# A delta-rule input projection in three-fold fp32r products, with the convolution over eight padded rows

## The reference, cut to what matters

```
def _dn_inputs(hn, n_rows, w_in, conv_w, a_log, dt_bias):
    z = hn @ w_in
    qkv = jax.nn.silu(_short_conv(z[..., :3 * DN_INNER], conv_w, n_rows))
    gate = z[..., 3 * DN_INNER:4 * DN_INNER]
    ba = z[..., 4 * DN_INNER:]
    ...
q, k, v, beta, g, gate = _dn_inputs(hn, n_rows, ...)       # 4 rows of 64 tokens
qc, kc, vc, betac, gc, gatec = _dn_inputs(hcn, 1, ...)     # one row of 256 tokens
```

## Time and profile before

| | us |
|---|---|
| median of 3 runs (lowest, highest) | 2886.16 (2881.43, 2887.08) |
| the profiled execution | 2880.9 |
| its span | 2879.1 |
| stage `dn_proj`, first matmul to the barrier | 51.95 to 229.22 |
| TensorE busy over the span | 2587.9 (90%) |
| VectorE, ScalarE busy over the span | 1914.4 (66%), 1286.8 (45%) |
| mean granted TensorE clock over the span | 0.925 |

### The profile page before, as it was taken

The page is one execution under the profiler, slowest core; times in us unless marked ns, Lnnn a source line. Parts: engine busy times, 40 slices in busy tenths (PEclk is TensorE's granted clock), DMA queues, the critical chain, the costliest instruction groups (busy, mean ns, idle before and its releaser), DMA issues. The chain is left out here.

```text
span 2879.1 us, 46266 instructions
## 1 busy us (share of the span) xinstructions
PE 2587.9 (90%) x18362; PEld 2102.2 (73%) x18362; DVE 1914.4 (66%) x2914; ACT 1286.8 (45%) x1663; POOL 41.0 (1%) x77
## 2 busy tenths in 40 slices
PE   5996799979687999999999879789999698799996
PEld 3543699957155999999999777578888586688885
DVE  2654666645997666666666565468888663588886
ACT  2112344311055444444444345257777352477774
POOL 1000000000000000000000010000000100000000
PEclk8996899999699999999999979799999897799998
DMA  6205200033866555555555552259999530399994
GB/s 256 101 29 191 78 3 3 3 125 132 322 198 214 187 185 187 189 185 187 185 186 189 187 201 82 84 219 366 367 360 351 226 126 12 152 373 366 364 357 161
DMA packets 132128, 553.70 MB, mean 192 GB/s; under 512 B 11151, under 2 KB 13391, under 8 KB 106631
## 3 DMA queue, kind: packets, MB, share of 16 engines
q1 hardware_dynamic: 126814, 532.79, 50.3%
q0 software_dynamic: 5168, 18.80, 1.9%
HBM read 549.37 MB, written 2.18 MB: 192 GB/s over the span
## 5 line engine op out<-in xcount | busy, mean ns | idle before, releaser
L254 PE MATMUL PS<-over,over 128*128 128x512 f32 (+1 forms) x2816 | 978.9, 348 | 29.9 <-DVE over L1731 11.2
L255 PE MATMUL PS<-over,over 128*128 128x512 f32 (+1 forms) x2816 | 970.9, 345 | 0.0
L256 PE MATMUL PS<-over,over 128*128 128x512 f32 (+1 forms) x2816 | 970.1, 344 | 0.0
L254 PEld LDWEIGHTS PS<-over,over 128*128 128x128 f32 x2816 | 538.9, 191 | 93.7 <-issue 20.6
L2624 DVE TENSOR_TENSOR over<-ring,over 128x2048 fp32r<-128x2048 f32 x240 | 548.8, 2291 | 77.5 <-ACT over L2565 76.5
L256 PEld LDWEIGHTS PS<-over,over 128*128 128x128 f32 x2816 | 538.0, 191 | 63.0
L255 PEld LDWEIGHTS PS<-over,over 128*128 128x128 f32 x2816 | 539.0, 191 | 59.9 <-issue 0.5
L2565 ACT CAST over<-ring 128x2048 fp32r<-128x2048 f32 x240 | 457.6, 1913 | 37.1 <-PE PS L256 36.7
L1731 DVE TENSOR_TENSOR over<-ring,over 128x1024 fp32r<-128x1024 f32 x256 | 312.8, 1223 | 105.7 <-ACT over L1704 105.7
L1704 ACT CAST over<-ring 128x1024 fp32r<-128x1024 f32 x256 | 267.4, 1046 | 177.5 <-PE PS L256 176.7
L1711 ACT ACTIVATE ring<-PS 128x256 f32<-128x256 f32 x128 | 49.2, 384 | 235.5 <-PE PS L256 235.5
(11 more groups left out here) (437 smaller groups left out, 2642.9 us busy)
## 6 DMA issues: line engine op xcount, KB each, us to landing
ring<-in_w_gate SPq DMA_DIRECT2D x80, 1024.0 KB, 4.9
ring<-in_w_up SPq DMA_DIRECT2D x80, 1024.0 KB, 7.2
ring<-in_w_down SPq DMA_DIRECT2D x80, 1024.0 KB, 7.7
ring<-in_mod_w SPq DMA_DIRECT2D x64, 1024.0 KB, 8.1
ring<-in_peer_u SPq DMA_DIRECT2D x128, 512.0 KB, 3.4
ring<-in_peer_v SPq DMA_DIRECT2D x128, 512.0 KB, 4.1
ring<-in_w_in SPq DMA_DIRECT2D x12, 2048.0 KB, 12.2
ring<-in_dn_w SPq DMA_DIRECT2D x8, 2048.0 KB, 7.9
```

The costliest lines, as they stand in the source:

```text
L254: nc.tensor.matmul(out, lhs[0], rhs[0], start=start, stop=False)
L255: nc.tensor.matmul(out, lhs[0], rhs[1], start=False, stop=False)
L256: return nc.tensor.matmul(out, lhs[1], rhs[0], start=False, stop=stop)
```

## The change

The stage's products, except ba, become `exact3`. For that, hnT is split once, in four quarters (`hnhi`, `hnlo`), and each weight slot in four units of two k-slices, 32 units in all, through three buffers `dn_whi` and three `dn_wlo`. ScalarE makes the high part of unit u when TensorE has used unit u - 3; VectorE makes the low part; TensorE runs a unit's products for all four tiles of the slot (two k-slices x four tiles), or for both token tiles of a gate slot. The slots come in the order k, k, v, v, q, q, gate, gate. A slot is free once VectorE has subtracted from its last quarter. Tiles are counted m in the new order, four to a slot, in eight PSUM banks; those of slot p wait until the middle tap of the tile that had the bank two slots before is made. ba stands behind unit 27.

The context is convolved as four rows of 64 too: zpad has eight rows of 68, and the two values beyond each inner edge of the context are copied from the neighbouring row. ScalarE makes the middle tap from PSUM into `conv`, with the tap as its scale; VectorE adds the four others over all eight rows at once. In iteration u ScalarE casts unit u and pads tile u - 6, and VectorE subtracts unit u and does the taps of tile u - 7.

The removed loops are those printed above; of the diff the new lines stand here, and the removed lines of the buffers:

```diff
-        XPAD = ROWS * (ROW_W + 2 * DN_PAD)
-        CPAD = T + 2 * DN_PAD
-        zpad = arena(16384, 2, XPAD + CPAD)
-        conv = arena(16384 + 2 * (XPAD + CPAD), 2, 2 * T)
+        ZROW = ROW_W + 2 * DN_PAD
+        zpad = arena(16384, 2, 2 * ROWS, ZROW)
+        conv = arena(16384 + 4 * ROWS * ZROW, 2, 2 * T)
...
-        first_w = ring_loads(io["dn_w"], 8)
+        DN_SL = (2, 3, 4, 5, 0, 1, 6, 7)
+        tiles = [4 * s + i for s in DN_SL[:6] for i in range(4)]
+        NTILE, NUNIT = len(tiles), 32
+        first_w = len(free_at)
+        for s in DN_SL:
+            ring_load(io["dn_w"][s])
...
-        dn1_pe = steps("pe", [("z", n) for n in range(24)] + rows_ev + ["ba"])
-        dn1_ac = steps("act", [x for n in range(24) for x in ([("pad", n)] + ([("silu", n - 1)] if n else []))] +
-                       [("silu", 23)] + rows_ev)
-        dn1_dv = steps("dve", ["zero"] + [("conv", n) for n in range(24)] + ["ba"])
-        for s in range(6):
-            free_at[first_w + s] = (dn1_pe, ("z", 4 * s + 3))
-        for s in range(2):
-            free_at[first_w + 6 + s] = (dn1_pe, ("row", s, NT - 1))
+        s_dwhi, s_dwuse, s_dhi, s_dlo = (sem("dn_" + n) for n in ("whi", "wuse", "hi", "lo"))
+        dn1_pe = steps("pe", [("z", p) for p in range(6)] + rows_ev[0:2] + ["ba"] + rows_ev[2:])
+        dn1_ac = steps("act", [x for m in range(NTILE) for x in ([("silu", m - 2)] if m >= 2 else []) + [("pad", m)]] +
+                       [rows_ev[0], ("silu", 22), rows_ev[1], ("silu", 23)] + rows_ev[2:])
+        dn1_dv = steps("dve", ["zero"] + [("conv", m) for m in range(NTILE)] + ["ba"])
+        dn1_lo = Steps(sem("dn_wlo"), list(range(NUNIT)))
+        for p in range(8):
+            free_at[first_w + p] = (dn1_lo, 4 * p + 3)
+        dn_whi = [r32(w, 2, CW) for w in (RB + 30720, RB + 31744, RB + 23552)]
+        dn_wlo = [r32(w, 2, CW)[0] for w in (RB + 8192, RB + 9216, hT_at)]
+        hnhi = [r32(RB + 19456 + 2 * CW * q, 2, 2 * T) for q in range(4)]
+        hnlo = [r32(RB + 26624 + 2 * CW * q, 2, 2 * T)[0] for q in range(4)]
+        def dn_toks(m):
+            return T if tiles[m] < DN_H else 2 * T
+        def dn_raw(u):
+            return slot(first_w + u // 4)[:, 2 * (u % 4):2 * (u % 4) + 2, :]
+        def dn_used(e, u):
+            if u % 4 == 3:
+                dn1_pe.wait(e, ("z", u // 4) if u < 24 else ("row", u // 4 - 6, NT - 1))
+            else:
+                e.wait_ge(s_dwuse, u // 4 * 3 + u % 4 + 1)
...
+            for u in range(NUNIT):
+                p, q = u // 4, u % 4
+                if u < 4:
+                    e.wait_ge(s_dlo, u + 1)
+                dn1_lo.wait(e, u)
+                w = dn_whi[u % 3][0], dn_wlo[u % 3]
+                for k2 in range(2):
+                    k = 2 * q + k2
+                    for i in range(4 if p < 6 else NT):
+                        bank = PS[:, 4 * (p % 2) + i, :]
+                        if k == 0 and p >= 2:
+                            dn1_ac.wait(e, ("pad", 4 * (p - 2) + i))
+                        if p < 6:
+                            toks, cs = dn_toks(4 * p + i), slice(i * P, (i + 1) * P)
+                            ins = exact3(bank[:, 0:toks], (w[0][:, k2, cs], w[1][:, k2, cs]),
+                                         (hnhi[q][0][:, k2, 0:toks], hnlo[q][:, k2, 0:toks]), k == 0, k == KC - 1)
+                        else:
+                            tk = slice(i * P, (i + 1) * P)
+                            ins = exact3(bank, (hnhi[q][0][:, k2, tk], hnlo[q][:, k2, tk]), (w[0][:, k2, :], w[1][:, k2, :]),
+                                         k == 0, k == KC - 1)
+                            if k == KC - 1:
+                                dn1_pe.mark(ins, ("row", p - 6, i))
+                if q < 3:
+                    ins.then_inc(s_dwuse, 1)
+                elif p < 6:
+                    dn1_pe.mark(ins, ("z", p))
+                if u == 27:
+                    e.wait_ge(s_dnin, 32)
+                    dn1_ac.wait(e, ("pad", 18))
+                    for t in range(NQ):
+                        for k in range(KC):
+                            ins = nc.tensor.matmul(PS[:, 2, t * 32:(t + 1) * 32], hnT[:, k, t * P:(t + 1) * P], wba[:, k, :],
+                                                   start=(k == 0), stop=(k == KC - 1))
+                    dn1_pe.mark(ins, "ba")
             return dn1_pe
...
+            A = nc.scalar
+            def silu(m):
+                dn1_dv.wait(e, ("conv", m))
...
+                dn1_ac.mark(A.activation(dest[:, n % DN_H, :], conv[:, m % 2, 0:dn_toks(m)], ACT.Silu), ("silu", m))
+            def pad(m):
+                dn1_pe.wait(e, ("z", m // 4))
+                if m >= 2:
+                    dn1_dv.wait(e, ("conv", m - 2))
+                bank, z, toks = PS[:, 4 * (m // 4 % 2) + m % 4, :], zpad[:, m % 2], dn_toks(m)
+                A.copy(z[:, 0:toks // ROW_W, DN_PAD:DN_PAD + ROW_W], bank[:, 0:toks].rearrange("p (r w) -> p r w", w=ROW_W))
+                if toks > T:
+                    inner = bank[:, T + ROW_W:2 * T].rearrange("p (r w) -> p r w", w=ROW_W)
+                    outer = bank[:, T:2 * T - ROW_W].rearrange("p (r w) -> p r w", w=ROW_W)
+                    A.copy(z[:, ROWS + 1:2 * ROWS, 0:DN_PAD], outer[:, :, ROW_W - DN_PAD:ROW_W])
+                    A.copy(z[:, ROWS:2 * ROWS - 1, DN_PAD + ROW_W:ZROW], inner[:, :, 0:DN_PAD])
+                if m >= 2:
+                    dn1_ac.wait(e, ("silu", m - 2))
+                dn1_ac.mark(A.activation(conv[:, m % 2, 0:toks], bank[:, 0:toks], ACT.Copy,
+                                         scale=cw[:, tiles[m], DN_PAD:DN_PAD + 1]), ("pad", m))
+            def gate_row(s, t):
+                dn1_pe.wait(e, ("row", s, t))
+                dn1_ac.mark(A.activation(gate[:, t, s * CW:(s + 1) * CW], PS[:, 4 * s + t, :], ACT.Silu), ("row", s, t))
+            for u in range(NUNIT):
+                if u < 4:
+                    A.copy(hnhi[u][0], hnT[:, 2 * u:2 * u + 2, :]).then_inc(s_dhi, 1)
+                if u % 4 == 0:
+                    ring_wait(e, first_w + u // 4)
+                if u >= 3:
+                    dn_used(e, u - 3)
+                A.copy(dn_whi[u % 3][0], dn_raw(u)).then_inc(s_dwhi, 1)
+                if u == 5:
+                    e.wait_ge(s_dnin, 32)
+                    dn1_dv.wait(e, "zero")
+                if 8 <= u < 30:
+                    silu(u - 8)
+                if 6 <= u < 30:
+                    pad(u - 6)
+                if u >= 30:
+                    gate_row(0, u - 30)
+                    silu(u - 8)
+            for t in range(NT):
+                gate_row(1, t)
...
+            V = nc.vector
+            def taps(m):
+                dn1_ac.wait(e, ("pad", m))
+                toks = dn_toks(m)
+                o = conv[:, m % 2, 0:toks].rearrange("p (r w) -> p r w", w=ROW_W)
+                for j in (0, 1, 3, 4):
+                    ins = V.scalar_tensor_tensor(o, zpad[:, m % 2, 0:toks // ROW_W, j:j + ROW_W], cw[:, tiles[m], j:j + 1], o,
+                                                 ALU.mult, ALU.add)
+                    if j == DN_TAPS - 1:
+                        dn1_dv.mark(ins, ("conv", m))
+                    else:
+                        c(ins)
+            for u in range(NUNIT):
+                if u < 4:
+                    e.wait_ge(s_dhi, u + 1)
+                    V.tensor_tensor(hnlo[u], hnT[:, 2 * u:2 * u + 2, :], hnhi[u][1], ALU.subtract).then_inc(s_dlo, 1)
+                e.wait_ge(s_dwhi, u + 1)
+                dn1_lo.mark(V.tensor_tensor(dn_wlo[u % 3], dn_raw(u), dn_whi[u % 3][1], ALU.subtract), u)
+                if u == 4:
+                    dn1_dv.mark(V.memset(zpad, 0.0), "zero")
+                if 7 <= u < 31:
+                    taps(u - 7)
             dn1_pe.wait(e, "ba")
-            dn1_dv.mark(nc.vector.tensor_copy(ba, PS[:, 0, 0:NQ * 32].rearrange("p (t c) -> p t c", t=NQ)), "ba")
+            dn1_dv.mark(V.tensor_copy(ba, PS[:, 2, 0:NQ * 32].rearrange("p (t c) -> p t c", t=NQ)), "ba")
```

More of the change, by code:

```diff
@@ L578, in pe_dn1 @@
         def pe_dn1(e, c):
[L579 to L603, removed]
-            return dn1_pe
-        def pad_views(buf):
-            return (buf[:, 0:XPAD].rearrange("p (r w) -> p r w", r=ROWS), buf[:, XPAD:XPAD + CPAD])
+            for u in range(NUNIT):
[32 more added lines that the diff above has]
+                    dn1_pe.mark(ins, "ba")
@@ L609, in act_dn1 @@
+            return dn1_pe
         def act_dn1(e, c):
[L610 to L614, removed]
+            A = nc.scalar
+            def silu(m):
+                dn1_dv.wait(e, ("conv", m))
+                n = tiles[m]
                 dest = (qT, kT, vT)[n // DN_H]
-                dn1_ac.mark(nc.scalar.activation(dest[:, n % DN_H, :], conv[:, n % 2, 0:toks], ACT.Silu), ("silu", n))
@@ L635, in act_dn1 @@
+            for t in range(NT):
+                gate_row(1, t)
             return dn1_ac
         def dve_dn1(e, c):
```

(15 more changed lines are left out.)

## The result

The changed kernel took 2863.99 us (median of 4 runs, 2862.76 to 2865.87), the kernel before 2884.44 beside it (4 runs, 2881.43 to 2887.08). The ratio is 0.9932 with an interval of 0.9918 to 0.9945: 0.7% faster, inside the predicted 2858 to 2876 and 3 us under the predicted 2867. The profiled execution took 2864.16 us, its span 2862.4. The stage carries the gain.

A forecast was written before the change was run, and what follows sets the result against it. TensorE was taken to bound 16 units, VectorE the next ten, then ba. The stage's end, 146.95 + 62.9 = 209.85 instead of 229.22, saves 19.4 us: 2886.2 - 19.4 = 2867, range 2858 to 2876.

The forecast's parts named there:

- The bound: In the stage before the change, TensorE is full, busy 176.85 of 177.4 us; VectorE and ScalarE have room.
- Start: Before the stage's first product, cast and subtraction take 3.9 us; the low clock then loses 2.3 us.
- VectorE and ScalarE: Per iteration, VectorE takes 4.2 us, or 3.1 with a query tile; ScalarE takes 2.8 us and is covered.
- E(15): End of the 16 key and value units, forecast at 146.95 us, with TensorE taking 5.55 us a unit.
- The stall: In unit 20 TensorE waits for a PSUM bank some 3.2 us, going on at about 15.7 after E(15).
- a clock under 1.0 between 160 and 185: Sign that the forecast is wrong, costing up to 2.3 us for each unit.
- ba and behind it: From 38.5 us after E(15): ba 10.1, four units of 2.77, clock loss 2.3, last SiLU and barrier 0.9.
- The sum: The stage ends at 209.85 instead of 229.22, 19.4 us less; median 2886.2 - 19.4 = 2867.
- The clock at 1.2 GHz from unit 20 on: Rival: the clock stays low from unit 20's stall to the stage's end, +26.1 us, 2893; chance 0.03.
- Costly taps: Rival: VectorE's taps cost twice today's, 1.03 us, so iterations 18 to 22 take 5.2 more: 2872; chance 0.10.
- The shorter gap: Rival: TensorE's gap is shorter with weights stationary, 5.9 us less in the first 16 units: 2861; chance 0.06.
- A hidden wait: Rival: a wait such as TensorE stopping in each slice for PSUM banks eats 10 us: 2877; chance 0.07.

The follow-up runs named there:

- Experiment 2: The kernel before with only the new convolution (eight padded rows, middle tap on ScalarE), products still fp32: stage 177.37 us, 2881.86 us, ratio 0.9996.
- experiment 1: The changed kernel's three-fold products, but five taps on VectorE in halves as in the kernel before: stage 172.59 us, 2874.72 us, ratio 0.9979.
- experiment 5: The changed kernel itself run again, unaltered (also called the repeat): stage 155.43 us, 2863.79 us, ratio 0.9939.
- experiment 4: The changed kernel with ba moved from unit 27 to behind the last unit: stage 154.32 us, 2866.43 us, ratio 0.9942.
- experiment 9: The changed kernel with each of four taps as two 256-element operations on key and value tiles: stage 159.47 us, 2863.82 us, ratio 0.9937.
- experiment 10: The changed kernel with all five taps on VectorE over eight rows, the first a multiplication: stage 161.86 us, 2868.46 us, ratio 0.9954.

## Why the prediction was right, step by step

**The bound.** Right. Experiment 2 takes 28 us off VectorE and moves nothing, experiment 1 takes TensorE's work down and is stopped by VectorE.

**Start.** The first product was predicted 3.9 us into the stage and came at 56.09, 3.77. The key and value units ended at about 146.3 (the cast behind them starts at 146.33), 94.0 us into the stage; 95.0 were predicted. A unit took 5.44 us ((147.41 - 87.58)/11), so a product 0.2266 us, not the 0.2311 of the earlier trace rows; by that the 16 units are 1.7 us shorter. The Trainium skill (TensorE: Matmul & The Clock Gate, Back-to-back issue gap) has 216 ns for 512 columns alone, and says that in a stream of weight loads and matmuls 131 ns are sustained: the trace agrees with neither, being 11 ns above the one and 96 above the other. The clock at the start took back part of the 1.7: it was at 1.2 GHz from the first product to 62, some 6 us, of which half is lost: 3.0 us instead of 2.3.

**VectorE and ScalarE.** Right within 0.04 us (the lower bound of a tap, 0.70, was added up wrong: half of 1.286 and the gap of 0.03 are 0.67; nothing hangs on it): iterations of 4.16 and 3.09 us against 4.2 and 3.1. On ScalarE the two small copies took 0.06 us each from start to start, and an iteration some 2.65 us against 2.8. The 18th to 22nd iterations ended 21.9 us after E(15) against 22.05, the subtraction of unit 27 at 35.5 against 35.7.

**The stall.** Right in place, cause and size: 3.01 us, ending 15.6 us after E(15), against 3.2 and 15.7. Its clock was not in the sum: it fell there in one profile of the changed kernel and not in the other. The prediction had named a clock under 1.0 between 160 and 185 as a sign of being wrong, at up to 2.3 us for each unit. The sign came, for 6.8 us in the first profile, and cost 1.3 us in all.

**ba and behind it.** ba began 39.7 us after E(15) against 38.5, since the clock stayed low behind the stall, until 168.0; in the repeat without that fall it was 183.70 - 145.31 = 38.4. It took 8.29 us against 10.1, since in this execution the clock held to 192. This is the worst-sized term of the sum, and the experiments show that it goes with the moment of the fall: 5.9 us into ba and 8.3 us, 4.0 and 10.1 (experiment 4), 3.0 and 10.9 (experiment 5). Units 28 to 31 and the tail took 208.16 - 194.33 = 13.8 us against 14.3, the first 4 or so at the low clock.

**The sum.** 94.0 + 61.8 = 155.8 us against 157.9. Its four errors are 1.0 us less up to E(15), 1.2 more up to ba, 1.8 less in ba and 0.5 less behind it. That they partly cancel is luck, and where the clock fell in this one execution is in at least three of them. The stage gained 21.1 us by the clock of the trace and 21.5 by its length, 19.4 predicted. The medians differ by 20.45 us (17.5 in experiment 5), the two profiled spans only by 16.7. Of the 3 us by which the median lies under the predicted 2867, 1.7 are the kernel before, which came out at 2884.44 beside it and not at 2886.16. The 4.4 us between the two profiles' 21.1 and 16.7 lie in the later stages, whose code is the same. One place is a window of 25 us in a later stage, here for the changed kernel in its two profiles, the first one above:

```profile
455.00:480.00 25.00, 24.14 (x401) 23.72 (x396) 10.99 (x25) 5.31 (x12) 0.00 (x0) 0.86 0.01 3
```

```profile
455.00:480.00 25.00, 24.15 (x438) 23.47 (x434) 13.92 (x30) 5.92 (x14) 0.00 (x0) 1.00 0.01 2
```

The same stretch, 0.86 of the clock in the one and 1.00 in the other. The rest took 2641.2 to 2652.7 us in the three profiles with a stage over 170 us, and 2648.4 to 2662.5 in the nine others. With that scatter it stays open whether a shorter stage loses a few us later.

**The rivals.** The clock at 1.2 GHz from unit 20 on did not come: it was back at 168, while TensorE had no more pauses, and 1.00 from 168 to 191. It was low for 6.8 us, a little longer than the 6 us within which the prediction saw it come back. Costly taps: 750 ns, not 1.03 us, and experiment 9 shows that they would have cost 3.6 us of stage, 5.1 up to ba (5.2 argued). The shorter gap came by some 0.0045 of the 0.015 us that the rival had: 0.2266. A hidden wait would have shown in TensorE's waits, where only the start and the stall stand; products alone (experiment 1) do have such waits, eight of ten of them for VectorE.

## What to carry to other kernels

Count for each kind of unit the time of each engine in an iteration, the lag of the trailing engine included: here the engine behind is seven tiles late, so its long tiles fall beside the leader's short units, and the order of the slots alone is worth 6 us. Two edits that each look nearly worthless (0.0 and 4.8 us), one that frees the idle engine and one that shortens the full one, can be worth 21 us together: cost them as a pair. Make small products wide before moving them about: ba as 24 products of 512 columns gave 4.35 us of stage, its move to the end 1.5.

## What was not expected of the hardware

- In ba's run of 64 records of 32 columns, TensorE busy without a pause, the clock fell to 1.2 GHz in each profile that has it, 3 to 6 us after it began; where products follow it came back 6.8 to 13.7 us later. With the same sums as wide products the clock stayed at 1.00. ba's length, 8.3 to 11.1 us, goes with that.
- At TensorE's pause of 3.0 us the clock fell in one execution and not in another of the same kernel, nor in experiment 4; at those of 4.6 (experiment 9), 3.5 (experiment 10) and 2.8 and 4.7 us (experiment 1) it fell too.
- On ScalarE two copies of six elements are 165 and 177 ns long, but the next operation starts 0.06 us after each.
- A tap over eight rows with gaps between them costs what the straight line between 256 elements (485 ns, in four rows with gaps too) and 1024 (1286 ns) gives, 750 ns for 512 elements; two of 256 took 2 x 0.516 from start to start.
